# Norm sums behind five rows, a filler ahead of the first cross score, head scaling ahead of a filler

## The reference, cut to what matters

```
xn = rmsnorm(x, g_mix);  one input projection -> attention q, k, v; mLSTM q, k, v, gates; convolution b, c, h
o_a = rmsnorm per head of (softmax(q1 k1) - lam * softmax(q2 k2)) v      # 4 heads of 128, differential attention
h_m = rmsnorm per head of the mLSTM's output                            # 4 heads of 64
x   = x + W_out [o_a | h_m | o_c]
x   = x + CrossAttn_4heads(rmsnorm(x, g_cross))                          # 256 memory tokens, heads of 256
x   = x + (silu(xn W_gate) * (xn W_up)) W_down,  xn = rmsnorm(x, g_ffn)
```

## Time and profile before

| | |
|---|---|
| median of 3 runs | 1831.57 us (1830.93 to 1833.03) |
| the profiled execution | 1837.14 us, of which the span from its first to its last instruction is 1835.2 us |
| PE busy | 1774.2 us, 97% of the span |
| DVE busy | 941.0 us, 51% |
| ACT busy | 592.9 us, 32% |
| mean granted TensorE clock | 0.990 |

### The profile page before, as it was taken

One profiled execution on the slowest core, in us unless ns is written; L12 is line 12 of the kernel. 1 busy time (PEld: TensorE's weight loads), 2 busy tenths in 40 slices (PEclk: granted clock), 3 DMA queues, 4 the chain that ended last, 5 costly groups with the idle time before them and its releaser, 6 DMA issues.

```text
span 1835.2 us, 33632 instructions
## 1 busy us (share of the span) xinstructions
PE 1774.2 (97%) x14360; PEld 1701.7 (93%) x14360; DVE 941.0 (51%) x2074; ACT 592.9 (32%) x1037; POOL 21.0 (1%) x22
## 2 busy tenths in 40 slices
PE   6999999999999999999999889999999999999996
PEld 6999889998899999999999888899889999999996
DVE  5674776544454434434566557755445443443444
ACT  4311344523332212212432124543333322222222
POOL 0100000000000000000010000000000000000000
PEclk9998999999999999999999999999999999999998
DMA  5222424224122222222332342242332232222232
GB/s 199 81 59 65 84 84 149 82 80 128 60 75 90 93 90 83 93 84 90 116 97 68 50 73 77 94 138 81 98 104 69 81 93 93 81 93 93 81 93 82
DMA packets 55690, 166.27 MB, mean 91 GB/s; under 512 B 10616, under 2 KB 13432, under 8 KB 55288
## 3 DMA queue, kind: packets, MB, share of 16 engines
q1 hardware_dynamic: 55544, 164.14, 29.7%
HBM read 152.92 MB, written 11.15 MB: 89 GB/s over the span
## 4 chain that ended last, share of the span: by engine, by line
PE 89%; DVE 6%; ACT 2%; issue 2%; another core or an unknown queue 0%; DMA 0%; DVEq 0%; SPq 0%; ACTq 0%
PE proj L766 25%; PE proj L768 24%; PE proj L769 24%; PE work L957 2%; PE work L944 2%; PE work L973 2%; DVE w_lo L1213 1%; PE proj L756 1%; PE proj L757 1%; PE proj L758 1%; PE work L921 1%; PE work L811 1%; PE work L546 1%; PE work L932 1%; PE proj L761 1%
## 5 line engine op out<-in xcount | busy, mean ns | idle before, releaser
L769 PE MATMUL proj<-xg_hi,w_hi 128*128 128x272 f32 x1664 | 445.5, 286 | 0.0
L768 PE MATMUL proj<-xg_lo,w_hi 128*128 128x272 f32 x1664 | 445.1, 286 | 0.0
L1213 DVE TENSOR_TENSOR w_lo<-raw,w_hi 128x1024 fp32r<-128x1024 f32 (+1 forms) x269 | 324.6, 1207 | 125.3 <-ACT w_hi L1013 124.5
L768 PE MATMUL proj<-xn_lo,w_hi 128*128 128x272 f32 x1376 | 375.0, 291 | 0.0
L769 PE MATMUL proj<-xn_hi,w_hi 128*128 128x272 f32 x1376 | 374.3, 291 | 0.0
L766 PE MATMUL proj<-xg_hi,w_lo 128*128 128x272 f32 x1664 | 346.3, 289 | 2.3 <-DVE w_lo L1213 2.3
L1013 ACT ACTIVATE w_hi<-raw 128x1024 fp32r<-128x1024 f32 (+1 forms) x269 | 277.6, 1036 | 169.8 <-PE proj L769 169.6
L768 PEld LDWEIGHTS proj<-xg_lo,w_hi 128*128 128x128 f32 x1664 | 312.6, 188 | 0.0
L769 PEld LDWEIGHTS proj<-xg_hi,w_hi 128*128 128x128 f32 x1664 | 312.5, 188 | 0.0
L766 PE MATMUL proj<-xn_hi,w_lo 128*128 128x272 f32 x1376 | 297.4, 298 | 13.9 <-DVE w_lo L1189 11.2
L768 PEld LDWEIGHTS proj<-xn_lo,w_hi 128*128 128x128 f32 x1376 | 263.3, 191 | 0.0
(11 more groups left out here) (281 smaller groups left out, 1864.1 us busy)
## 6 DMA issues: line engine op xcount, KB each, us to landing
raw<-in_weights SPq DMA_DIRECT2D x270, 512.0 KB, 3.5
xT<-in_x SPq DMA_DIRECT2D x4, 544.0 KB, 6.1
out_k_fm<-kh SPq DMA_DIRECT2D x8, 272.0 KB, 4.2
out_y_fm<-y SPq DMA_DIRECT2D x8, 272.0 KB, 2.4
out_p_att_v<-vtok_a SPq DMA_DIRECT2D x8, 256.0 KB, 3.5
out_mk_fm<-mkT SPq DMA_DIRECT2D x8, 256.0 KB, 4.2
xkT<-in_mem_kT SPq DMA_DIRECT2D x8, 256.0 KB, 3.3
xv<-in_mem_v SPq DMA_DIRECT2D x8, 256.0 KB, 3.8
```

The costliest lines, as they stand in the source:

```text
L768: mm(pb[h][:, 0:HALF], wh, xl[:, a:b], start=False, stop=False)
L769: last = mm(pb[h][:, 0:HALF], wh, xh[:, a:b], start=False, stop=final)
L1213: v.tensor_tensor(w_lo[:, s, 0:nt, :], raw[:, r, 0:nt, :], w_hi[:, s, 0:nt, :].bitcast(F32), ALU.subtract).then_inc(split_lo, 1)
```

## The change

Three edits of the list of steps; no computation is added or dropped. In `cuts`, the sums of a wide norm stand behind five rows k of the tile that follows, where they stood behind three, and `norm` behind seven (the first layer's `gates` keeps its cuts). The finished heads 4, 5, 0, 1 and 2 are scaled (`f_scale`) at the end of a phase's own steps, ahead of its filler, and no longer behind a filler. The cross attention gets an empty phase ahead of its first, so that the first half of `cq` 2 stands ahead of the first `x_score`, and the six halves of its first three fillers stand one to a phase.

```diff
--- before.py
+++ after.py
@@ -100,7 +100,7 @@
     steps = []
 
 
-    cuts = {("gates", 0): [0, 3, 6, KT], ("cq", 0): [0, 3, 6, KT], ("gate", 0): [0, 3, 6, KT],
+    cuts = {("gates", 0): [0, 5, 7, KT] if l else [0, 3, 6, KT], ("cq", 0): [0, 5, 7, KT], ("gate", 0): [0, 5, 7, KT],
             ("out", 0): [0, 3, KT - 1, KT], ("out", 1): [0, KT - 1, KT], ("co", 0): [0, 2, 4, 6, KT], ("co", 1): [0, 2, 4, 6, KT]}
 
     def tile(kind, j):
@@ -169,7 +169,8 @@
 
     jobs = [(h, i) for h in range(H_A) for i in range(NQ + 1)]
     phases = []
-    finish = {0: [("f_square", 4)], 1: [("f_sum", 4)], 2: [("f_scale", 4), ("f_square", 5)], 3: [("f_sum", 5)], 4: [("f_scale", 5)]}
+    finish = {0: [("f_square", 4)], 1: [("f_sum", 4)], 2: [("f_square", 5)], 3: [("f_sum", 5)]}
+    scale = {3: 4, 5: 5}
     for n in range(len(jobs) + 3):
         ph, behind = [], []
         if 1 <= n <= len(jobs):
@@ -181,11 +182,13 @@
             if jobs[n - 3][1] == NQ:
                 ph.append(("f_square", jobs[n - 3][0]))
                 finish[n] = [("f_sum", jobs[n - 3][0])]
-                finish[n + 1] = [("f_scale", jobs[n - 3][0])]
+                scale[n + 2] = jobs[n - 3][0]
         if 2 <= n < len(jobs) + 2:
             ph.append(("a_prob", jobs[n - 2]))
         if n < len(jobs):
             ph.append(("a_exp", jobs[n]))
+        if n in scale and scale[n] < H_A - 1 or n in (3, 5):
+            ph.append(("f_scale", scale[n]))
         behind += finish.get(n, []) if n < len(jobs) + 2 else []
         if n < len(jobs) and jobs[n][1] == 0 and jobs[n][0]:
             behind.append(("a_turn", jobs[n][0]))
@@ -230,7 +233,7 @@
         phases.append((ph, []))
     steps.extend(tile("cq", 1))
     for h in range(H_X - 1):
-        weave(phases[(NQ + 1) * h:(NQ + 1) * (h + 1)], CROSS_FILL[h])
+        weave([([], [])] * (h == 0) + phases[(NQ + 1) * h:(NQ + 1) * (h + 1)], CROSS_FILL[h])
 
     rest = [ph for ph, _ in phases[(NQ + 1) * (H_X - 1):]]
     o0, o1 = tile("co", 0), tile("co", 1)
```

## The result

The changed kernel takes 1841.38 us (median of 5 runs, 1839.57 to 1845.19). The kernel before, run beside it on the same chip, takes 1832.1 us (1830.93 to 1835.39). The ratio is 1.0042, 95% interval 1.0023 to 1.006: slower by some 7.7 us by that ratio (the two medians differ by 9.3 us), where 1.0 us less was forecast.

What follows compares the result with a forecast made beforehand. The prediction took PE, busy 1774 of 1835 us, as the bound, so only PE's waits count. Terms -1.4 - 1.9 + 1.2 + 5.8 - 4.7 = -1.0 us gave 1830.6 us, range 1827.0 to 1834.5.

Steps and rivals of the forecast that it cites:

- Norm sums behind five rows: Wide norms: `ssum` waits of 0.69 us vanish; -1.4 us in two cq tiles, +1.2 us in three gates and gate tiles.
- The rival that Ln is held behind its table load anyway: Gates and gate tiles: later sums stay hidden, the three tiles cost nothing; -2.2 us, 1829.4 us; chance 0.04.
- Cross attention begins with a filler: Start of cross attention: the first score no longer waits for `qc`; -1.9 us in two layers.
- Finished heads scaled in front of a filler: Attention, five heads per layer: `a_mix` waits of 4.7 us removed, `f_scale` waits for ACT's copies of 5.8 us added.
- Net: +1.1 us, between -1.6 and +7.5: Moved scaling in the attention: 5.8 us of new `f_scale` waits against 4.7 us of `a_mix` waits removed.
- The slower rival: Attention: DVE's scaling is late behind a `w_lo`, so `a_mix` waits stay beside the new ones; +3.7 us, 1835.3 us; chance 0.12.
- The list of signs: Waits in the profile, at norms, first score, `a_mix` and `f_scale`, named beforehand as showing the forecast right or wrong.
- wrong: `f_scale` waits over 1 us: Attention: `f_scale` waits over 1 us, or under 0.35 us, or `a_mix` waits that stay, would show the forecast wrong.
- the signs named for "right": No `ssum`, first-score or `a_mix` waits; second gate tile about 2.3 us; Ln 0.4 us late; ten `f_scale` waits of 0.45-0.7 us.
- The sum: Whole kernel: -1.4 - 1.9 + 1.2 + 5.8 - 4.7 = -1.0 us, giving 1830.6 us; forecast's chance 0.61.
- upper end for the parts, +8.3: Whole kernel: the parts' ends add to -4.9 and +8.3 us; new `f_scale` waits reach 1.22 us each at the upper end.

Runs made afterwards that it cites:

- e_root1: The changed kernel with one Newton step instead of three in `f_sum`'s inverse root, leaving out part of the computation; 1835.77 us, ratio 0.9995 to the kernel before.
- e_order: The kernel before with only DVE's order changed: `w_lo` behind the scaling for heads 4, 1 and 2, `f_scale` where it was; ratio 0.9998.
- e_lo: The kernel before with `f_scale` in the middle of the filler it stood behind, and `w_lo` behind the scaling where both share a phase; ratio 0.9999.
- e_mid: The kernel before with `f_scale` moved into the middle of the filler behind which it stood; ratio 0.9986.
- e_best: The kernel before with `f_scale` mid-filler, `w_lo` behind it, the filler ahead of the first cross score, five rows in the cq tiles only; 1827.61 us, ratio 0.9957.

## Why the prediction was wrong, point by point

**Norm sums behind five rows: right in kind.** All five waits went. In the cq tiles each gave 0.91 us, where the row of the wait says 0.69. In the gates and gate tiles the wait of the next tile grew to 2.31 us ("about 2.3") and Ln came 0.24 us behind its table load (0.4 forecast), so the tiles cost 0.20 to 0.25 us each instead of 0.4. What was not forecast is the half clock behind the 2.31 us wait, 1.5 us where it falls.

The rival that Ln is held behind its table load anyway is refuted: with the sums later Ln waits 0.24 us for PE, and the load's end (523.89 + 1.28 = 525.17) holds it no longer than that. The drain of about 1.38 us that the Trainium skill gives ("ScalarE: Activation LUTs", section "What ACT_TABLE_LOAD costs") does not show in either kernel here: ACT is idle for 0.02 us ahead of the loads at these norms and for 0.01 us behind them in the kernel before.

**Cross attention begins with a filler: right,** -2.4 us for -1.9, and nothing turned up a phase later.

**Finished heads scaled in front of a filler: the step that failed,** "Net: +1.1 us, between -1.6 and +7.5". Heads 5, 0, 1 and 2 alone cost 5.7 us, the same in the run with this edit alone. By the forecast's terms these eight phases would have cost 0.69 x 2 + 0.58 x 6 - 4.7 = +0.2 us.

- The terms that it had were sound. The `a_mix` waits went, all but 0.5 us, and where DVE is not late `f_scale` waits 0.58 and 0.69 us as worked out from the earlier trace rows. With the short chain those heads cost 0.8 us (e_root1), 0.6 us more than the forecast's terms. A part of that can be overlap that the rows do not show: before, a projection follows the first of three transposes by 232.14 - 231.89 = 0.25 us, now `f_scale` follows by 235.49 - 234.34 = 1.15 us; 0.90 us are lost where the row says 0.66, since it counts from the modelled end of the transpose ahead.
- What was missing is one mechanism, 4.9 us by the same run: the working priced what the moved matmuls would wait for in their new place, and never asked what they had covered in the old one. They stood between `f_sum`, which gives DVE its root chain, and the `a_score` after the next one, which needs DVE to have read two banks behind that chain. The earlier trace rows show no `a_score` wait because of them. A wait that does not exist yet has no row; it is found by taking the moved work out of the timeline and asking of each step behind it whether its operand would be ready that much earlier.
- The slower rival (scaling still in front of `a_mix`) was the wrong one as well: `a_mix` is not where the time went. It did name DVE's `w_lo` ahead of the scaling, which e_order and e_lo show to be what held `a_mix` longest before (head 2).
- The list of signs did only half of its work: "wrong: `f_scale` waits over 1 us" came up at head 4 (1.01 us), though head 4 scatters. But the signs named for "right" came up too, nearly all of them, and the list had none for a new wait at a step that was not moved.

**The sum.** By the trace the parts are -4.3 (cross attention), +0.7 (three norm tiles), +1.5 (half clock), +5.7 (four heads) and, as an estimate, +1.5 for head 4 at the price of head 5 (0.75 us a layer): +5.1 us, inside the measured 4.2 to 11.0 us (0.0023 and 0.006 of 1832.1), though 2.6 us short of its middle. The forecast's upper end for the parts, +8.3, holds the measured value too, but only by `f_scale` waits of 1.22 us each, which did not come.

## What to carry to other kernels

Before work is moved on the engine that sets the time, ask two things of it: what it will wait for in the new place, and which wait of another step it hides in the old one, by looking at what the other engines do during it. When a wait names an engine, look at the order of that engine's queue first: with PE's matmuls done earlier `a_mix` still waited 1.22 us for head 2 (e_mid), and with `w_lo` moved behind the scaling on DVE as well it did not wait (e_lo). A wait that is given back a tile later can cost more than it saves, here 0.2 us a tile and the clock now and then.

## What the runs showed of the hardware

**A longer stop can cost the clock, but need not.** In the five kernels with the late sums in the gate tiles, PE stands for 2.31 us ahead of the second gate tile, ten times in all; 6 times the next 62 projection matmuls' starts then span 9.4 us instead of 7.8, with rows at the lower of the two clock levels (0.55 granted over 3.5 us above), 4 times not. In the seven kernels with a wait of 1.2 us there, it fell 0 times of 14. What decides between the 6 and the 4 stays open.

**Some stops have no releaser on the core.** In the last kernel (e_best), head 4 of the first layer, DVE:

```profile
189.05 0.24 DVE L1560 SCALAR_TENSOR_TENSOR mq<-mq,par,work 128x32 f32<-128x32 f32 x1
192.00 0.75 DVE L1560 SCALAR_TENSOR_TENSOR mq<-mq,par,work 128x512 f32<-128x512 f32 x1 [2.71 <-remote]
```

and ACT, at the same time:

```profile
192.13 0.38 ACT L1029 ACTIVATE mkT<-proj 128x256 f32<-128x256 f32 x1 [1.65 <-remote]
```

Two engines stop in the middle of a step and go on within 0.13 us of each other. The list of DMA queues from 188 to 193 us shows one packet of an instruction queue beside the loads of weights:

```profile
q8 instruction: 1, 0.02, 1.3%
```

In all twelve profiles, the stops of over 0.1 us that are put down to "remote" lie around the beginning of a layer's attention, from 189 to 199 us or from 1076 to 1096 us, up to 8.5 us each. Head 4 lies there, and it scatters by some us from run to run; the mLSTM's stage scatters as well, without such a stop. That the engines wait there for their instructions is a reading and not shown: such packets stand also where no engine stops so (two from 300 to 320 us in the changed kernel), and no run without the loads was made. Scatter of this size can hide a gain of 3 us in the time, as in e_lo.
